# Block 1's output product cut into pieces of one contraction tile between the mLSTM heads, with the gate sums and first scores moved into the last attention unit

## The chip, the cores and the metric

The kernel runs on one NeuronCore of one Trainium2 chip. The metric is the device time of one execution in microseconds, the median of several runs. The engines are TensorE (matmuls, PE in the profile), VectorE (DVE), ScalarE (ACT), GpSimd (POOL) and SyncE (SP), which issues the DMAs of the weights. Each engine executes its own instructions in the order in which they are written; between engines there are only counting semaphores.

## The reference: two blocks, of which the first matters here

The input is one sequence of 256 tokens of width 1024. Block 1 is a hybrid layer, cut here to its core:

```
proj = rms_norm(x, g_mix_pre) @ w_in      # q,k,v of 8 attention heads; q,k,v,o and two gates of 4 mLSTM heads
att  = moba_attention(rope(aq), rope(ak), av)                  # causal softmax, 256 tokens
hm   = mlstm_chunkwise(q_m, k_m, v_m, ig, lf)                  # 4 heads of value width 128
hm   = rms_norm_per_head(hm) * g_mlstm_out * sigmoid(mo)
mixed = concat([att, hm])                                      # 512 + 512 columns
x = x + rms_norm(mixed @ w_out, g_mix_post)
u = square(relu(rms_norm(x, g_mlp_pre) @ w_up)); x = x + rms_norm(u @ w_down, g_mlp_post)
```

Block 2 (two layers with modulation by `ada_w`, differential attention, a convolution and a gated MLP) follows. The change leaves it as it is.

## The kernel before: how the work is laid out

**Weights.** All big products are float32 in three passes: a weight chunk of up to four contraction tiles (128 x 4 x 512, 1 MB) is loaded into `raw`, ScalarE writes its rounded high part `hi` (function `split` of ScalarE, line 797), VectorE writes the rest `lo` (`split` of VectorE, line 1115), and TensorE multiplies hi*hi, lo*hi and hi*lo (line 422). The three buffers form a ring of three slots, so `split` of chunk c waits until the product of chunk c-3 is finished (semaphore `mm_done`), and is called two chunks ahead of use (`LEAD = 2`). A chunk is 4 contraction tiles x 4 output tiles x 3 passes = 48 matmuls. The output product `mixed @ w_out` is chunks 12 to 15: 12 and 13 hold the contraction tiles of the attention half for output columns 0 to 511 and 512 to 1023 (the "halves" of the output), 14 and 15 those of the mLSTM half. Chunks 16 and later belong to `w_up`.

**Attention units.** Eight heads ("units", the loop `for i in range(UNITS + 1)`) go through a pipeline: `scores` (PE into bank 0), `softmax_max` (DVE), `exps` (ACT), `probs` (DVE), `turn` (PE transposes into bank 1), `take_turned` (ACT copies bank 1), `apply_v` (PE into bank 2), a copy (DVE, line 1335), `high` (ACT, `att_hi`) and `low_of_heads` (DVE, `att_lo`). The chunks of the input projection fill the units 0 to 6; units 7 and 8 have none.

**mLSTM heads.** For each of four heads h:

- `m_scores(h)`, PE: one matmul broadcasts the gate rows into bank 1 (line 624), two form the scores in bank 0 (lines 628 and 629).
- `m_exps(h)`, ACT: copy of bank 1 (`bcA`), then, after DVE's `m_args(h)`, the exponentials `sA` and `emA`.
- `m_weights(h)`, DVE: mask and product with the scores, lines 1351 and 1352.
- `m_sums(h)`, PE: four matmuls into bank 2, lines 637 to 640.
- `m_out(h)`, DVE: lines 1361 to 1364, ending in `hmA`. It frees bank 2.
- `m_norm(h)`, ACT, and `head_squares()`, PE (line 553): the square, its sum over the head, then Ln and Exp (`rstd`), later `act_hi` (line 863).
- `m_final(h)`, DVE: lines 1370 and 1374, then `act_lo` (line 1163).

On DVE the loop runs `m_args(h+1)`, `m_weights(h+1)`, `m_out(h)`, `m_final(h-1)`. On ACT it runs `m_exps(h+1)`, `m_norm(h-1)`. Before the change, TensorE does the whole chunk 12 after the sums of head 0, and chunk 13 after those of head 3; ScalarE and VectorE `split` chunks 14 and 15 at the same two places (`fill_at = {0: 0, MH: 1}`). Then come the chunks 14 and 15.

**What follows the product.** On ACT: `split(16)`, `split(17)`, then the squares of the output product (`post_norm`). On DVE: `split(16)`, one piece of the modulation product (`ada_piece`, lines 1134 and 1136), `split(17)`, another such piece, then `add_squares` (line 1394). On PE: `sum_squares_late` (lines 501 and 506) waits for `add_squares`; then four warm-up matmuls, the norm of `x`, and the product with `w_up`.

```
            for c in groups[("out", 0)][1][1:] + groups[("out", 1)][1][1:]:
                advance(c)
            post_norm("out", pcols("g_mix_post"))
```

Of the kernel before, what the change touches and what calls it, by code (L numbers as in the profile page):

```python
# [25 lines left out]
P = 128  # L26
S = 256
TT = S // P
# [4 lines left out]
CK = 4  # L33
RING = 3
LEAD = 2
EPS = 1e-6
EPS_SUB = 1e-5
QK = 64
# [132 lines left out]
def two_blocks(nc, t, consts, out):  # L171
# [48 lines left out]
    with ExitStack() as ctx:  # L220
# [8 lines left out]
        def sem(name):  # L229
            if name not in sems:  # L230
                sems[name] = nc.alloc_semaphore(name)
            return sems[name]
# [106 lines left out]
        fill_at = {0: 0, MH: 1}  # L339
# [49 lines left out]
        def _(pe):  # L389
# [209 lines left out]
            for i in range(UNITS + 1):  # L599
                if i < len(todoA):  # L600
                    name, j = todoA[i]
                    chunk(name, j, act_hi, act_lo, token_major=name in (("in", 2), ("in", 4)))
                if i + 1 < UNITS:
                    scores(qk1, i + 1)
                if i < UNITS:
                    turn(pA[:, i % 2, :])
                u = i - 1
                if u == 0:
                    pe.wait_ge(sem(freed(("in", 2))[0]), freed(("in", 2))[1])
                if u >= 0:  # L610
                    apply_v(ptA[:, u % 2, :], v1, u * QK, QK, QK * (u % 2), u % 2 == 1)


            wait("gate_rows_ready")
            b = bank(0)
            for tt in range(TT):
                ins = pe.transpose(b[:, 4 * tt:4 * tt + 4], gate[:, 5, tt * P:tt * P + P], ident[0:4, 0:4])
            full(ins, 0)
            for g in (3, 4):
                pe.wait_ge(sem(freed(("in", g))[0]), freed(("in", g))[1])  # L620

# [20 lines left out]
            m_scores(0)  # L642
            for h in range(MH + 1):
                if h + 1 < MH:
                    m_scores(h + 1)
                if h < MH:
                    m_sums(h)
                if h in fill_at:
                    chunk(("out", fill_at[h]), 0, att_hi, att_lo, ready=None if fill_at[h] else "act_ready")
                if h:  # L650
                    head_squares()

            for half in range(2):
                chunk(("out", half), 1, act_hi, act_lo, ready=None if half else "act_ready")
# [123 lines left out]
        def _(act):  # L778
# [132 lines left out]
            for i in range(UNITS + 1):  # L911
                if i < len(todoA):
                    name, j = todoA[i]
                    split(groups[name][1][j] + LEAD)
                if i + 1 < UNITS:
                    exps(i + 1, sA, pA)
                if i < UNITS:
                    take_turned(ptA[:, i % 2, :])
                if i < len(todoA) and j == 1:
                    if name[1] == 2:  # L920
                        evacuate(name, v1[:, :, :])
                    elif name[1] == 3:
                        evacuate(name, mqk[:, :, :])
                    elif name[1] == 4:
                        evacuate(name, mv[:, :, :])
                if i >= 2 and i % 2 == 0:
                    h = i // 2 - 1
                    high(hf[:, h % 2, :], att_hi[:, h, :], "of_ready", "act_hi_ready")

# [15 lines left out]
            m_exps(0)  # L945
            evacuate(("in", 5), mo[:, :, :], other(ACT.Tanh), 0.5)
            for h in range(MH + 1):
                if h in fill_at:
                    split(groups[("out", fill_at[h])][1][0] + LEAD)
                if h + 1 < MH:  # L950
                    m_exps(h + 1)
                if h:
                    m_norm(h - 1)
# [139 lines left out]
        def _(dve):  # L1093
# [227 lines left out]
            for i in range(UNITS + 1):  # L1321
                if i < UNITS:
                    probs(i, pA)
                if i == 0:
                    gate_rows()
                if i < len(todoA):
                    name, j = todoA[i]
                    advance(groups[name][1][j])
                if i + 1 < UNITS:
                    softmax_max(i + 1, sA)  # L1330
                if i % 2 == 1 and i >= 3:
                    low_of_heads(i // 2 - 1)
                if i >= 2 and i % 2 == 0:
                    h = i // 2 - 1
                    v(dve.tensor_copy(hf[:, h % 2, :], full(2)[:, 0:S]), "bank2_free")
                    v.settle()
                    dve.sem_inc(sem("of_ready"), 1)
            low_of_heads(UNITS // 2 - 1)
            link(dve.tensor_copy(acol[:].rearrange("p t h -> p (t h)"), full(0)[:, 0:8]), "bank0_free")

# [37 lines left out]
            m_args(0)  # L1378
            m_weights(0)
            for h in range(MH + 1):  # L1380
                if h in fill_at:
                    split(groups[("out", fill_at[h])][1][0] + LEAD)
                if h + 1 < MH:
                    m_args(h + 1)
                    m_weights(h + 1)
                if h < MH:
                    m_out(h)
                if h:
                    m_final(h - 1)
# [211 lines left out]
```

## Time and profile before

| | us |
|---|---|
| median of 3 runs | 1171.54 |
| lowest, highest | 1170.97, 1173.06 |
| the profiled execution, its time | 1168.2 |
| the profiled execution, its span | 1166.4 |
| PE busy / DVE busy / ACT busy in the span | 1113.2 / 815.4 / 525.8 |
| mean granted clock of TensorE | 0.981 of full speed |

The span runs from the first to the last instruction; the rest of the execution's time (1.8 us) lies around it. TensorE is busy nearly all the time, so what a change is worth is read where TensorE waits or runs at a lower granted clock. The part that the change touches lies between 115 and 190 us.

### The profile page before, as it was taken

The page shows a single profiled execution, that of the slowest core. Times are in us where ns is not written, and L with a number is a line of the kernel's source. Part 1 is how long each engine was busy: PE and PEld are TensorE (multiplying, and loading weights), DVE is VectorE, ACT ScalarE, POOL GpSimd, SP SyncE. Part 2 cuts the span into 40 slices and gives each one's busy share as a digit, 9 for nine tenths or more (in the row PEclk, how much of TensorE's full clock was granted, in tenths as well). Part 3 has the DMA queues.
Part 4 walks back from the last instruction along what each step waited for, and adds up shares of the span by engine and source line. Part 5 has one row for each costly group of instructions (what it writes and reads, how often), then busy time and mean ns, then how long its engine had stood idle before and what let it go on. Part 6 is the DMA issues. An engine that isn't in the chain of part 4 may idle for free.

```text
span 1166.4 us, 19617 instructions
## 1 busy us (share of the span) xinstructions
PE 1113.2 (95%) x8436; PEld 1049.9 (90%) x8436; DVE 815.4 (70%) x1089; ACT 525.8 (45%) x605; POOL 12.1 (1%) x26
## 2 busy tenths in 40 slices
PE   5999888999999899989999999999998999999998
PEld 5878677999999798978999999999897899999998
DVE  5965677777665799864788787768989277566452
ACT  4544445565333534544553434345346255444432
POOL 4000000000000000000000000000000000000000
PEclk8999889999999999989999999999999999999998
DMA  6543233887987154413879998955442275676550
GB/s 209 181 130 129 103 111 105 297 304 267 329 296 242 62 191 146 145 37 129 287 247 308 325 295 317 333 179 182 159 157 82 72 235 192 223 231 204 184 177 37
DMA packets 131494, 228.61 MB, mean 196 GB/s; under 512 B 5925, under 2 KB 59539, under 8 KB 131409
## 3 DMA queue, kind: packets, MB, share of 16 engines
q1 hardware_dynamic: 130404, 227.11, 57.8%
q8 instruction: 66, 1.08, 0.4%
q0 software_dynamic: 672, 0.06, 0.1%
q10 hardware_dynamic: 333, 0.21, 0.1%
q14 instruction: 19, 0.16, 0.0%
HBM read 226.30 MB, written 1.05 MB: 195 GB/s over the span
## 4 chain that ended last, share of the span: by engine, by line
PE 72%; DVE 19%; ACT 5%; issue 3%; DMA 1%; DVEq 0%; SPq 0%; ACTq 0%
PE mm L422 63%; DVE cacc L1195 5%; DVE lo L1115 5%; ACT hi L797 3%; PE pv L479 2%; PE mm L461 1%; DVE ada_acc L1136 1%; PE pa L506 1%; DVE sB L1203 1%; DMA raw<-in_w_out_dram 1%; DVE hf L1409 1%; DVE pB L1492 1%; PE pa L493 1%; DVE qk L1219 0%; DVE x L1414 0%
## 5 line engine op out<-in xcount | busy, mean ns | idle before, releaser
L422 PE MATMUL mm<-act_hi,hi 128*128 128x256 f32 x1760 | 491.6, 283 | 9.4 <-ACT act_hi L859 6.7
L422 PE MATMUL mm<-act_hi,lo 128*128 128x256 f32 x1760 | 486.0, 280 | 0.0
L1115 DVE TENSOR_TENSOR lo<-raw,hi 128x2048 fp32r<-128x2048 f32 (+1 forms) x160 | 361.8, 2265 | 172.1 <-ACT hi L797 170.8
L422 PE MATMUL mm<-act_lo,hi 128*128 128x256 f32 x1760 | 468.4, 279 | 0.0
L797 ACT ACTIVATE hi<-raw 128x2048 fp32r<-128x2048 f32 (+1 forms) x160 | 301.4, 1889 | 217.8 <-PE mm L422 167.4
L422 PEld LDWEIGHTS mm<-act_hi,hi 128*128 128x128 f32 x1760 | 332.0, 189 | 15.7 <-issue 8.9
L422 PEld LDWEIGHTS mm<-act_hi,lo 128*128 128x128 f32 x1760 | 332.0, 189 | 0.8 <-issue 0.7
L422 PEld LDWEIGHTS mm<-act_lo,hi 128*128 128x128 f32 x1760 | 321.0, 188 | 0.0
L422 PE MATMUL mm<-u_hi,hi 128*128 128x256 f32 x608 | 170.3, 280 | 0.0
L422 PE MATMUL mm<-u_hi,lo 128*128 128x256 f32 x608 | 169.7, 279 | 0.0
L422 PE MATMUL mm<-u_lo,hi 128*128 128x256 f32 x608 | 169.6, 279 | 0.0
L422 PEld LDWEIGHTS mm<-u_hi,lo 128*128 128x128 f32 x608 | 114.3, 188 | 0.0
L422 PEld LDWEIGHTS mm<-u_hi,hi 128*128 128x128 f32 x608 | 114.3, 188 | 0.0
L422 PEld LDWEIGHTS mm<-u_lo,hi 128*128 128x128 f32 x608 | 114.3, 188 | 0.0
L1136 DVE SCALAR_TENSOR_TENSOR ada_acc<-ada_raw,ca,ada_acc 128x1024 f32<-128x1024 f32 x84 | 107.6, 1280 | 1.3 <-DVE ada_acc L1136 0.3
L1195 DVE SCALAR_TENSOR_TENSOR cacc<-cu,convw,cacc 128x256 f32<-128x256 f32 x240 | 98.9, 477 | 2.4
L1163 DVE TENSOR_TENSOR u_lo<-sq,u_hi 128x512 fp32r<-128x512 f32 (+1 forms) x30 | 25.0, 834 | 35.2 <-ACT u_hi L983 18.6
L1066 ACT ACTIVATE sq<-mm 128x512 f32<-128x512 f32 x22 | 13.1, 597 | 61.0 <-PE mm L422 61.0
L422 PE MATMUL mm<-on,raw 128*128 128x256 f32 x128 | 33.5, 421 | 7.5 <-DVE on L1498 7.5
L422 PEld LDWEIGHTS mm<-on,raw 128*128 128x128 f32 x128 | 27.2, 215 | 12.7 <-issue 8.2
L870 ACT ACTIVATE pB<-sB,small 128x128 f32<-128x128 f32 (+1 forms) x32 | 14.3, 449 | 50.4 <-DVEq L1207 50.4
L863 ACT ACTIVATE u_hi<-sq 128x512 fp32r<-128x512 f32 x22 | 13.9, 632 | 44.5 <-DVEq L1552 44.5
(245 smaller groups left out, 976.5 us busy)
## 6 DMA issues: line engine op xcount, KB each, us to landing
ada_raw<-in_ada_w_dram SPq DMA_DIRECT2D x96, 512.0 KB, 5.9
raw<-in_w_ffn_in_dram SPq DMA_DIRECT2D x88, 512.0 KB, 5.8
raw<-in_w_in_dram SPq DMA_DIRECT2D x40, 1024.0 KB, 5.1
raw<-in_w_ffn_out_dram SPq DMA_DIRECT2D x20, 1024.0 KB, 6.3
raw<-in_w_up_dram SPq DMA_DIRECT2D x16, 1024.0 KB, 6.3
raw<-in_w_down_dram SPq DMA_DIRECT2D x16, 1024.0 KB, 7.3
raw<-in_w_out_dram SPq DMA_DIRECT2D x12, 1024.0 KB, 5.1
raw<-in_w_in_dram SPq DMA_DIRECT2D x16, 512.0 KB, 5.2
```

The lines of the kernel that those rows point to most:

```text
L422: ins = pe.matmul(o, w[:, kk, fs], a[:, k, :], start=(k == 0 and i == 0 and f % 2 == 0), stop=(ends and i == len(pairs) - 1), skip_group_c ...
L461: ins = pe.matmul(mm[:, b0 + tt, :], a[:, k, tok], w[:, kk, :], start=(k == 0 and i == 0), stop=(ends and i == 2), skip_group_check=True)
L479: ins = pe.matmul(b[:, f:f + 1], ada_acc[:, i % 2, f * P:(f + 1) * P], ones[:, 0:1], start=(f == 0), stop=True, skip_group_check=True)
L493: ins = pe.matmul(pa[:, 0:S], ones, sq[:, k, :], start=(k == 0), stop=(k == KD - 1))
L797: a(act.activation(hi[:, c % RING, 0:nk, :], raw[:, c % RING, 0:nk, :], ACT.Copy), "hi_done")
L863: a(act.activation(dst, src, ACT.Copy, scale=scale), done)
L870: a(act.activation(p[:, i, lo_:hi_], s[:, i, lo_:hi_], ACT.Exp, scale=-1.0, bias=small[:, 2 + 2 * i + q:3 + 2 * i + q], accum_out=small[:, ...
L1066: a(act.activation(sq[:, 0:2, :], complete((l, "ffn", g))[:, 0, :], other(ACT.Silu)), "silu_gate_ready")
L1115: v(dve.tensor_tensor(lo[:, c % RING, 0:nk, :], raw[:, c % RING, 0:nk, :], hi[:, c % RING, 0:nk, :].bitcast(F32), ALU.subtract), "lo_done")
L1136: link(dve.scalar_tensor_tensor(out=acc, in0=w, scalar=ca[:, 1, k:k + 1], in1=acc, op0=ALU.mult, op1=ALU.add), "ada_used")
L1163: ins = dve.tensor_tensor(d_lo, src, h, ALU.subtract)
L1195: v(dve.scalar_tensor_tensor(out=cacc[:, k, :], in0=src, scalar=w, in1=cacc[:, k, :], op0=ALU.mult, op1=ALU.add), name)
```

## The change

TensorE: in the last attention unit, after `turn(7)`, it now does the gate transposes, and `m_scores(0)`, ahead of both `apply_v` calls; between these stands the first piece of the output product. `out_piece(half, j, ks)` does contraction tiles `ks` of chunk 12 + half + 2j, 12 matmuls each. The remaining pieces stand between the heads, and the two mLSTM chunks alternate tile by tile. ScalarE and VectorE split chunk 14 in the last attention unit and chunk 15 after `m_exps(3)` and `m_weights(3)`. ScalarE does `m_exps(0)` ahead of `high` of the last attention pair; VectorE does the copies of the gate sums (`acol`) and `m_args(0)` ahead of the copy of that pair, and `m_weights(0)` behind it. What comes behind the product is unchanged.

```diff
-        fill_at = {0: 0, MH: 1}
...
+            def out_piece(half, j, ks):
+
+                name = ("out", half)
+                g, ids = groups[name]
+                slot, acts = ids[j] % RING, ((att_hi, att_lo), (act_hi, act_lo))[j]
+                if 0 in ks:
+                    begin(name, j)
+                for kk in ks:
+                    if half == 0:
+                        wait("act_ready")
+                    ends = j == 1 and kk == CK - 1
+                    for tiles in ((0, 1), (2, 3)):
+                        ins = tile_products(2 * (g % 2), slot, kk, CK * j + kk, tiles, acts, ends)
+                        if ends and half and tiles[0] == 0:
+                            ins.then_inc(sem("half_done"), 1)
+                if CK - 1 in ks:
+                    ins.then_inc(sem("mm_done"), 1)
+
             for i in range(UNITS + 1):
...
                 if i < UNITS:
                     turn(pA[:, i % 2, :])
+                if i == UNITS - 1:
+                    wait("gate_rows_ready")
+                    b = bank(0)
+                    for tt in range(TT):
+                        ins = pe.transpose(b[:, 4 * tt:4 * tt + 4], gate[:, 5, tt * P:tt * P + P], ident[0:4, 0:4])
+                    full(ins, 0)
+                    for g in (3, 4):
+                        pe.wait_ge(sem(freed(("in", g))[0]), freed(("in", g))[1])
+                    m_scores(0)
...
                     apply_v(ptA[:, u % 2, :], v1, u * QK, QK, QK * (u % 2), u % 2 == 1)
...
-            m_scores(0)
-            for h in range(MH + 1):
+                if i == UNITS - 1:
+                    out_piece(0, 0, (0,))
+
+            fill = [((0, 0, (1, 2)),), ((0, 0, (3,)), (1, 0, (0,))), ((1, 0, (1, 2)),), ((1, 0, (3,)), (0, 1, (0,)))]
+            for h in range(MH):
                 if h + 1 < MH:
                     m_scores(h + 1)
-                if h < MH:
-                    m_sums(h)
-                if h in fill_at:
-                    chunk(("out", fill_at[h]), 0, att_hi, att_lo, ready=None if fill_at[h] else "act_ready")
+                m_sums(h)
+                for piece in fill[h]:
+                    out_piece(*piece)
                 if h:
                     head_squares()
-
+            out_piece(1, 1, (0,))
             for half in range(2):
-                chunk(("out", half), 1, act_hi, act_lo, ready=None if half else "act_ready")
+                out_piece(half, 1, (1,))
+            head_squares()
+            for kk in (2, 3):
+                for half in range(2):
+                    out_piece(half, 1, (kk,))
...
                 if i + 1 < UNITS:
                     exps(i + 1, sA, pA)
+                if i == UNITS - 1:
+                    split(groups[("out", 0)][1][0] + LEAD)
                 if i < UNITS:
                     take_turned(ptA[:, i % 2, :])
+                if i == UNITS:
+                    m_exps(0)
...
             for h in range(MH + 1):
-                if h in fill_at:
-                    split(groups[("out", fill_at[h])][1][0] + LEAD)
                 if h + 1 < MH:
                     m_exps(h + 1)
+                if h == 2:
+                    split(groups[("out", 1)][1][0] + LEAD)
                 if h:
                     m_norm(h - 1)
...
                     low_of_heads(i // 2 - 1)
+                if i == UNITS:
+                    split(groups[("out", 0)][1][0] + LEAD)
+                    link(dve.tensor_copy(acol[:].rearrange("p t h -> p (t h)"), full(0)[:, 0:8]), "bank0_free")
+                    m_args(0)
                 if i >= 2 and i % 2 == 0:
                     h = i // 2 - 1
                     v(dve.tensor_copy(hf[:, h % 2, :], full(2)[:, 0:S]), "bank2_free")
                     v.settle()
                     dve.sem_inc(sem("of_ready"), 1)
+
+            m_weights(0)
             low_of_heads(UNITS // 2 - 1)
...
             for h in range(MH + 1):
-                if h in fill_at:
-                    split(groups[("out", fill_at[h])][1][0] + LEAD)
                 if h + 1 < MH:
                     m_args(h + 1)
                     m_weights(h + 1)
+                if h == 2:
+                    split(groups[("out", 1)][1][0] + LEAD)
                 if h < MH:
                     m_out(h)
```

Where two places of the program stand, in the order of instructions on an engine (line numbers differ between the two versions). First TensorE in the last attention unit, before; `cst,pA` is `turn(7)`, `ptA,v` are `apply_v(6)` and `apply_v(7)`, `cst,gate` the gate transposes, `gate,cst` and `mqk` are `m_scores`:

```order
L538 MATMUL pv<-cst,pA 128x128 [waits bank1_free,probs_ready]
L538 MATMUL pv<-cst,pA 128x128 x2
L545 MATMUL pv<-ptA,v 64x256 [waits bank2_free,bank1_free]
L546 MATMUL pv<-ptA,v 64x128
L545 MATMUL pv<-ptA,v 64x256 [waits bank1_free]
L546 MATMUL pv<-ptA,v 64x128
L617 MATMUL pv<-cst,gate 128x4 [waits bank0_free,gate_rows_ready]
L617 MATMUL pv<-cst,gate 128x4
L624 MATMUL pv<-gate,cst 128x512 [waits bank1_free,group_free0,group_free1]
L628 MATMUL pv<-mqk 128x256 [waits bank0_free]
L629 MATMUL pv<-mqk 128x128
```

The same place in the change:

```order
L537 MATMUL pv<-cst,pA 128x128 [waits bank1_free,probs_ready]
L537 MATMUL pv<-cst,pA 128x128 x2
L648 MATMUL pv<-cst,gate 128x4 [waits bank0_free,gate_rows_ready]
L648 MATMUL pv<-cst,gate 128x4
L600 MATMUL pv<-gate,cst 128x512 [waits bank1_free,group_free0,group_free1]
L604 MATMUL pv<-mqk 128x256 [waits bank0_free]
L605 MATMUL pv<-mqk 128x128
L544 MATMUL pv<-ptA,v 64x256 [waits bank2_free,bank1_free]
L545 MATMUL pv<-ptA,v 64x128
L421 MATMUL mm<-att_hi,hi 128x256 [waits act_ready,lo_done,group_free0]
```

The gate transposes and the scores of head 0 have moved ahead of both `apply_v`, and the first piece of the output product (its first row is the last one shown) stands between these.

VectorE around the outputs of heads 2 and 3, before; `lo<-raw,hi` is `split`, `hmA` ends `m_out`, `cols,rstd` begins `m_final`:

```order
L1352 SCALAR_TENSOR_TENSOR pA<-pv,sA 128x384 [waits bank0_full,dve_step]
L1361 TENSOR_TENSOR hf<-pv,emA 128x256 [waits bank0_free,bank2_full]
L1362 SCALAR_TENSOR_TENSOR hf<-pv,hf 128x256 [waits dve_step]
L1363 RECIPROCAL hf<-hf 128x256 [waits dve_step]
...
L1163 TENSOR_TENSOR act_lo<-hf,act_hi 128x256 [waits act_hi_ready]
L1115 TENSOR_TENSOR lo<-raw,hi 128x2048 [waits hi_done,act_ready]
L1370 SCALAR_TENSOR_TENSOR hf<-hmA,cols,rstd 128x256 [waits rstd_ready]
L1374 SCALAR_TENSOR_TENSOR hf<-mo,hf 128x256 [waits group_free1,dve_step]
```

The same engine and place in the change:

```order
L1357 SCALAR_TENSOR_TENSOR pA<-pv,sA 128x384 [waits bank0_full,dve_step]
L1140 TENSOR_TENSOR lo<-raw,hi 128x2048 [waits bank0_free,hi_done]
L1366 TENSOR_TENSOR hf<-pv,emA 128x256 [waits bank2_full]
L1367 SCALAR_TENSOR_TENSOR hf<-pv,hf 128x256 [waits dve_step]
L1368 RECIPROCAL hf<-hf 128x256 [waits dve_step]
...
L1188 TENSOR_TENSOR act_lo<-hf,act_hi 128x256 [waits act_hi_ready]
L1375 SCALAR_TENSOR_TENSOR hf<-hmA,cols,rstd 128x256 [waits rstd_ready,act_ready]
L1379 SCALAR_TENSOR_TENSOR hf<-mo,hf 128x256 [waits group_free1,dve_step]
```

The split of chunk 15 has moved from ahead of the last `m_final` to between the weights of head 3 and `m_out(2)`.

## Rows read from the trace of the kernel before

**Rows 1.** The page's first line: the span.

```profile
span 1166.4 us, 19617 instructions
```

**Rows 2.** Windows: busy us (instructions) by engine, then granted clock, DMA share, GB/s.

```profile
119.50:122.50 3.00, 2.58 (x12) 1.24 (x12) 0.91 (x3) 1.28 (x3) 0.00 (x0) 1.00 0.30 122
126.50:129.00 2.50, 2.50 (x8) 2.12 (x8) 0.60 (x1) 2.35 (x3) 0.00 (x0) 0.50 0.00 0
143.50:156.00 12.50, 8.45 (x28) 6.65 (x27) 8.80 (x16) 4.54 (x11) 0.00 (x0) 0.50 0.00 1
174.00:188.00 14.00, 10.66 (x44) 7.80 (x44) 7.14 (x15) 4.65 (x9) 0.00 (x0) 1.00 0.37 134
...
899.50:903.40 3.90, 0.49 (x3) 0.09 (x1) 3.90 (x10) 3.66 (x5) 0.00 (x0) 0.68 0.00 0
903.40:906.00 2.60, 2.28 (x6) 1.86 (x7) 0.57 (x2) 0.03 (x1) 0.00 (x0) 0.50 0.00 0
```

**Rows 3.** Timeline of PE: start, us, line, tiles, [idle before, releaser].

```profile
122.66 0.70 PE L628 MATMUL pv<-mqk 64*128 64x256 f32 x2 [0.58 <-DVE acol L1339]
137.03 0.70 PE L637 MATMUL pv<-pA,mv 128*128 128x256 f32 x2
138.69 0.70 PE L553 MATMUL pa<-sq,cst 128*128 128x256 f32 x2
150.95 1.19 PE L637 MATMUL pv<-pA,mv 128*128 128x256 f32 x2 [3.02 <-DVE hmA L1364]
153.64 1.06 PE L553 MATMUL pa<-sq,cst 128*128 128x256 f32 x2
```

**Rows 4.** The chain that ended last, pieces in order of time: start, us, what.

```profile
154.70 6.68 PE mm L422 x48
161.81 5.62 PE mm L422 x48
173.88 1.10 PE pa L501 x4
174.99 1.74 PE pa L506 x8
```

**Rows 5.** Timeline of ACT.

```profile
119.50 0.49 ACT L874 ACTIVATE ptA<-pv 128x384 f32<-128x384 f32 x1 [0.83 <-PE pv L538]
161.84 0.48 ACT L833 ACTIVATE rstd<-pa,small 128x256 f32<-128x256 f32 x1 [1.09 <-PE pa L553]
163.78 0.42 ACT L863 ACTIVATE act_hi<-hf 128x256 fp32r<-128x256 f32 x1 [1.01 <-DVE hf L1374]
164.11 1.90 ACT L797 ACTIVATE hi<-raw 128x2048 fp32r<-128x2048 f32 x1
167.50 1.92 ACT L797 ACTIVATE hi<-raw 128x2048 fp32r<-128x2048 f32 x1 [1.49 <-PE mm L422]
```

**Rows 6.** Timeline of DVE.

```profile
147.67 0.42 DVE L1361 TENSOR_TENSOR hf<-pv,emA 128x256 f32<-128x256 f32 x1
150.38 0.42 DVE L1364 TENSOR_TENSOR hmA<-pv,hf 128x256 f32<-128x256 f32 x1
160.55 2.29 DVE L1115 TENSOR_TENSOR lo<-raw,hi 128x2048 fp32r<-128x2048 f32 x1 [1.45 <-ACT hi L797]
162.81 0.48 DVE L1370 SCALAR_TENSOR_TENSOR hf<-hmA,cols,rstd 128x256 f32<-128x256 f32 x1
166.11 2.29 DVE L1115 TENSOR_TENSOR lo<-raw,hi 128x2048 fp32r<-128x2048 f32 x1 [1.45 <-ACT hi L797]
168.32 0.75 DVE L1134 TENSOR_SCALAR ada_acc<-ada_raw,ca 128x1024 f32<-128x1024 f32 x1
169.53 2.29 DVE L1115 TENSOR_TENSOR lo<-raw,hi 128x2048 fp32r<-128x2048 f32 x1 [0.46 <-ACT hi L797]
171.74 1.28 DVE L1136 SCALAR_TENSOR_TENSOR ada_acc<-ada_raw,ca,ada_acc 128x1024 f32<-128x1024 f32 x1
173.05 0.69 DVE L1394 TENSOR_TENSOR sq<-sq 128x512 f32<-128x512 f32 x1
```

More of the change, by code:

```diff
@@ L598, in _ @@
             full(ins, 2)
[L599 to L620, printed above, removed]
             def m_scores(h):
@@ new lines, in _ @@
+            for i in range(UNITS + 1):
+                if i < len(todoA):
+                    name, j = todoA[i]
+                    chunk(name, j, act_hi, act_lo, token_major=name in (("in", 2), ("in", 4)))
+                if i + 1 < UNITS:
+                    scores(qk1, i + 1)
+                if i < UNITS:
+                    turn(pA[:, i % 2, :])
+                if i == UNITS - 1:
[7 more added lines that the diff above has]
+                    m_scores(0)
+                u = i - 1
+                if u == 0:
+                    pe.wait_ge(sem(freed(("in", 2))[0]), freed(("in", 2))[1])
+                if u >= 0:
+                    apply_v(ptA[:, u % 2, :], v1, u * QK, QK, QK * (u % 2), u % 2 == 1)
+                if i == UNITS - 1:
+                    out_piece(0, 0, (0,))
@@ L910, in _ @@
             a(act.activation(gate[:, 2, :], gate[:, 2, :], ACT.Ln, bias=1.0), "softplus_ready")
[L911 to L928, printed above, removed]
             def m_exps(h):
@@ L943, in m_norm @@
                 high(hf[:, h % 2, :], act_hi[:, 4 + h, :], "of_ready", "act_hi_ready")
-            m_exps(0)
+            for i in range(UNITS + 1):
+                if i < len(todoA):
+                    name, j = todoA[i]
+                    split(groups[name][1][j] + LEAD)
+                if i + 1 < UNITS:
+                    exps(i + 1, sA, pA)
+                if i == UNITS - 1:
+                    split(groups[("out", 0)][1][0] + LEAD)
+                if i < UNITS:
+                    take_turned(ptA[:, i % 2, :])
+                if i == UNITS:
+                    m_exps(0)
+                if i < len(todoA) and j == 1:
+                    if name[1] == 2:
+                        evacuate(name, v1[:, :, :])
+                    elif name[1] == 3:
+                        evacuate(name, mqk[:, :, :])
+                    elif name[1] == 4:
+                        evacuate(name, mv[:, :, :])
+                if i >= 2 and i % 2 == 0:
+                    h = i // 2 - 1
+                    high(hf[:, h % 2, :], att_hi[:, h, :], "of_ready", "act_hi_ready")
             evacuate(("in", 5), mo[:, :, :], other(ACT.Tanh), 0.5)
             for h in range(MH + 1):
-                if h in fill_at:
-                    split(groups[("out", fill_at[h])][1][0] + LEAD)
                 if h + 1 < MH:
                     m_exps(h + 1)
+                if h == 2:
+                    split(groups[("out", 1)][1][0] + LEAD)
                 if h:
@@ L1320, in _ @@
             link(dve.memset(gate[:, 7, :], 0.0))
[L1321 to L1339, printed above, removed]
             def m_args(h):
@@ L1376, in m_final @@
                 v.settle()
-            m_args(0)
+            for i in range(UNITS + 1):
+                if i < UNITS:
+                    probs(i, pA)
+                if i == 0:
+                    gate_rows()
+                if i < len(todoA):
+                    name, j = todoA[i]
+                    advance(groups[name][1][j])
+                if i + 1 < UNITS:
+                    softmax_max(i + 1, sA)
+                if i % 2 == 1 and i >= 3:
+                    low_of_heads(i // 2 - 1)
+                if i == UNITS:
+                    split(groups[("out", 0)][1][0] + LEAD)
+                    link(dve.tensor_copy(acol[:].rearrange("p t h -> p (t h)"), full(0)[:, 0:8]), "bank0_free")
+                    m_args(0)
+                if i >= 2 and i % 2 == 0:
+                    h = i // 2 - 1
+                    v(dve.tensor_copy(hf[:, h % 2, :], full(2)[:, 0:S]), "bank2_free")
+                    v.settle()
+                    dve.sem_inc(sem("of_ready"), 1)
             m_weights(0)
+            low_of_heads(UNITS // 2 - 1)
             for h in range(MH + 1):
-                if h in fill_at:
-                    split(groups[("out", fill_at[h])][1][0] + LEAD)
                 if h + 1 < MH:
```

## The prediction

> **What bounds the kernel now.** I read the page first, then the chain that ended last, then the timelines of the three engines around the change, then windows for the granted clock. The span is 1166.4 us [rows 1]. The chain is TensorE for most of its length, so outside the changed stretch every microsecond by which the product with `w_up` starts later should stay to the end.
>
> In the changed stretch TensorE doesn't bound. Between the heads it waits for VectorE: 3.02 us before the sums of head 3, until `hmA` of head 2 is written [rows 3]. And it runs at half clock: 0.50 from 126.5 to 129.0 and again from 143.5 to 156.0 [rows 2]. What half clock costs is read from pairs of equal work: the sums of a head take 1.66 us at full clock (137.03 to 138.69) and 2.69 us at half (150.95 to 153.64) [rows 3]; a chunk that begins at half clock takes 6.68 us, one at full clock 5.62 us [rows 4]. One piece of the change is a quarter of a chunk, 1.405 us at full clock.
>
> The place that decides is the end. The product ends at about 173.0 us, but the sum of squares starts at 173.88 [rows 4], and it is VectorE that it waits for. Followed back on VectorE without a hole above 0.5 us: `add_squares` at 173.05, modulation piece from 171.74, split of chunk 17 from 169.53, modulation piece from 168.32, split of chunk 16 from 166.11 [rows 6]; that split waits for ScalarE's half of it at 164.11, which runs behind `act_hi` of head 3 at 163.78 [rows 5], and this behind `m_final(3)` at 162.81 [rows 6]. So the sum of squares starts 173.88 - 162.81 = 11.07 us after `m_final(3)` starts, however early the product itself ends, as long as it ends in that time. The only slack in it is the 0.46 us that VectorE waits for the split of chunk 17 [rows 6], since ScalarE can begin that only when chunk 14's product is done (167.50 [rows 5]).
>
> **Step 1, the last attention unit.** ScalarE is free 0.83 us before its copy of bank 1 at 119.50 [rows 5], so at 118.67. Now the split of chunk 14 (1.90) is ahead of this copy (0.49): it ends at about 121.0. The gate broadcast on TensorE uses bank 1 and waits for it; TensorE is done with the transposes and gate transposes at 119.7 and idles 1.3 us. It then broadcasts (1.05). On VectorE the split of chunk 14 (2.2) stands ahead of the `acol` copy, so the scores of head 0 start at 123.0 where they started at 122.66 [rows 3]. What is queued behind them: both `apply_v` (0.8 each) and the first piece (1.4), and VectorE's copy of bank 2 waits for the second `apply_v`, with `m_weights(0)` behind that copy. Worked out: 123.0 + 0.86 + 0.8 + 1.4 + 0.8 = 126.9; copy 0.42 and weights 1.16: 128.6. The sums of head 0 begin about 3 us later than before. Most of it is given back, since the split of chunk 14 no longer stands between heads 0 and 1 on either engine: I find `m_out(0)` about 0.5 us late.
>
> **Step 2, the heads.** They stay a serial loop of VectorE and ScalarE, and pieces on TensorE don't shorten it. The split of chunk 15 now stands between `m_weights(3)` and `m_out(2)`. `m_out(2)` ran from 147.67 to 150.80; with the split's 2.2 us and some 0.7 us of waiting for ScalarE's half of it ahead, it ends at about 153.8. TensorE waits for it with the sums of head 3: start 153.9 instead of 150.95. What TensorE has ahead of that ends sooner: sums of head 2 from about 144.0 (1.66), two pieces (2.81), a short wait and the head sum of head 1 (0.63), to about 149.5. So it idles about 4.4 us.
>
> **Step 3, the last head's norm.** Before, the split of chunk 15 (160.55 plus 2.2) stood right ahead of `m_final(3)` [rows 6], and `rstd`, begun at 161.84 [rows 5], was ready at the same time. The split is gone from there, but the last head sum now comes late on TensorE: behind the sums of head 3 (1.66) stand two pieces (2.81), a head sum (0.63), three pieces (4.22) and the head sum itself (0.63): 153.9 + 9.95 = 163.85. From the start of Ln to `m_final(3)` it was 162.81 - 161.84 = 0.97 [rows 5, 6]: `m_final(3)` starts at 164.9 instead of 162.81, 2.1 us later.
>
> **Step 4, the end.** The product ends at about 163.85 + 4 x 1.405 = 169.5, some 3.5 us earlier than before. But the sum of squares starts at 164.9 + 11.07 - 0.46 = 175.5, which is 1.6 us **later**. (The 0.46 goes, since ScalarE's split of chunk 17 is finished at about 170.2, before VectorE asks for it.) TensorE idles about 6 us there, where it idled 0.9.
>
> **Step 5, the clock.** After the 3.7 us for which TensorE waits near 900 us the clock is 0.50 for the next 2.6 us and the stretch with the gap itself has a mean of 0.68 [rows 2]. Both new gaps (4.4 and 6 us) are longer. After the first, the sums of head 3 cost 2.69 - 1.66 = 1.03 more, and the following pieces 6.68 - 5.62 = 1.06 more; all of this is ahead of the last head sum: +2.1. After the second, the sum of squares, 2.84 us at full clock [rows 4], costs at the ratio 2.69 / 1.66 another 1.8, and a little of the warm-up matmuls behind it: +2.0. Bounds of this term: nothing, if the clock holds, and about +5 if half clock lasts into the first matmuls of `w_up`; I take 2.0, because before the clock was 1.00 from 174 to 188 with gaps of up to 1.7 us [rows 2], so it comes back there. In step 1 the half-clock stretch of before (126.5 to 129.0) delayed nothing, since VectorE's split came last; now one between 122 and 127 would delay `m_weights(0)` by 1.0. Bounds 0 and 1.0; I take 0.5.
>
> Part 4 of the Trainium skill's page TensorE: Matmul & The Clock Gate says that transposes don't count as activity for the clock in the way matmuls do. The stretch 119.5 to 122.5 of before kept 1.00 with `apply_v` and the broadcast in it [rows 2]; in the change transposes and the broadcast alone stand there, which no row of before shows. By that rule the last term would be 1.0 instead of 0.5, and the sum 6.7.
>
> **Sum:** 1.6 + 2.1 + 2.0 + 0.5 = +6.2 us on the profiled execution's 1168.2 (span 1166.4 plus 1.8 around it), so 1174.4. The median of the runs is 3.3 us above that execution; against it I forecast 1171.54 + 6.2 = **1177.7 us**. The DMAs give nothing: chunks 17 and 18 load earlier, behind splits that come earlier, but no wait for them lies on this chain. Work on TensorE is the same, matmul for matmul.
>
> **Rivals.** A measurement tells about 0.2% (2.3 us) from no change.
>
> - *The clock holds* (the pieces between heads keep TensorE busy enough, and the gaps are not long enough). Then only 1.6 us remain: 1173.1, within 0.2%. For it: pieces now stand in the stretch from 143.5 to 156. Against it: the gaps themselves grow. Chance 0.14.
> - *The early split of chunk 15 is hidden*, because ScalarE has done its half in time and the sums of head 3 start at 151: then `m_final(3)` starts about 161.9, the end is 1.4 us earlier, 1170.1 at full clock, still within 0.2%. The row of `m_out(2)` shows VectorE at work without a hole on both sides, so I give it 0.03.
> - *Faster: the sum of squares follows the product.* If VectorE's chain of two splits and two modulation pieces were not what the sum of squares waits for, the product's earlier end would count: -3.5 us, 1168.0. It decides from the point at which `m_final(3)` starts before 160.5. Against it: VectorE's chain was the later one already. Chance 0.05.
> - *Half clock lasts longer*, through the norm into the first chunks of `w_up`, or in two stretches among the heads: +9.5 us, 1181. The gaps of the norm (up to 1.7 us) come right behind the long one. Chance 0.18.
>
> My forecast has 0.60. The likeliest case alone: 1175 to 1180. The range takes in the held clock and most of the longest: 1173.0 to 1181.0. Faster 0.05; within 0.2% 0.17; slower 0.78.
>
> **What the profile of the change would show.** Right, if: PE idles over 5 us before the sum of squares (line of `sum_squares_late`), released by DVE's `sq` add; PE idles about 4 us before the sums of head 3, released by `hmA`; the last `m_final` starts near 165 to 168; the clock shows 0.50 after both gaps; and the product ends before the 173.0 of before, or about there where half clock hits it. Wrong, if ScalarE's split of chunk 14 doesn't hold up the broadcast, if the last head sum is done by 161, or if the clock stays 1.00 behind the gap at the end.

## The result, and the profile after

| | before | after |
|---|---|---|
| median | 1171.54 us (7 runs, 1170.97 to 1173.06) | 1179.77 us (7 runs, 1176.44 to 1182.02) |
| profiled execution, time and span | 1168.2, 1166.4 us | 1180.19, 1178.3 us |
| mean granted clock | 0.981 | 0.975 |

The ratio is 1.0067 with a 95% interval of 1.0051 to 1.0082: slower by 7.9 us. I had forecast 1177.7 us, range 1173.0 to 1181.0.

The page of the change; the instructions are as many as before, and PE is busy 7 us longer (1120.3 against 1113.2) with the same matmuls, which is the clock:

```profile
span 1178.3 us, 19617 instructions
PE 1120.3 (95%) x8436; PEld 1055.7 (90%) x8436; DVE 815.8 (69%) x1089; ACT 525.8 (45%) x605; POOL 12.0 (1%) x26
```

The five longest waits of PE from 118 to 181 us (total us, times, longest); before, over the same stretch of the program, the first was 0.9 us and the second 4.7 us in two times:

```profile
PE pa L500 <- DVE sq L1421: 5.7, 1, 5.7
PE pv L613 <- DVE hmA L1369: 4.5, 1, 4.5
PE pv L537 <- DVE pA L1330: 1.4, 1, 1.4
PE pv L600 <- ACT ptA L896: 0.9, 1, 0.9
PE pv L604 <- DVE pA L1357: 0.8, 1, 0.8
```

VectorE in the change, the rows that answer to [rows 6]:

```profile
156.94 0.42 DVE L1369 TENSOR_TENSOR hmA<-pv,hf 128x256 f32<-128x256 f32 x1
...
169.46 0.48 DVE L1375 SCALAR_TENSOR_TENSOR hf<-hmA,cols,rstd 128x256 f32<-128x256 f32 x1 [2.90 <-ACT rstd L857]
...
172.77 2.29 DVE L1140 TENSOR_TENSOR lo<-raw,hi 128x2048 fp32r<-128x2048 f32 x1 [1.45 <-ACT hi L819]
174.97 0.75 DVE L1159 TENSOR_SCALAR ada_acc<-ada_raw,ca 128x1024 f32<-128x1024 f32 x1
175.76 2.29 DVE L1140 TENSOR_TENSOR lo<-raw,hi 128x2048 fp32r<-128x2048 f32 x1
177.97 1.28 DVE L1161 SCALAR_TENSOR_TENSOR ada_acc<-ada_raw,ca,ada_acc 128x1024 f32<-128x1024 f32 x1
179.28 0.69 DVE L1421 TENSOR_TENSOR sq<-sq 128x512 f32<-128x512 f32 x1
```

The reader is to see two things. Behind the last `m_final` (169.46) VectorE works without a hole to the add of squares, except for the wait for ScalarE's half of chunk 16 that it had before; and the second split no longer waits. TensorE had ended the product at 174.4 and starts the sum of squares at 180.12:

```profile
157.51 1.19 PE L613 MATMUL pv<-pA,mv 128*128 128x256 f32 x2 [4.46 <-DVE hmA L1369]
...
180.12 2.04 PE L500 MATMUL pa<-sq,cst 128*128 128x256 f32 x4 [5.68 <-DVE sq L1421]
181.96 3.02 PE L505 MATMUL pa<-sq,cst 128*128 128x256 f32 x8
```

Windows of the change: the last unit, the sums of head 3, the gap at the end with the sum of squares behind it (the last figures are granted clock, DMA share, GB/s):

```profile
120.50:129.40 8.90, 8.03 (x24) 5.12 (x24) 3.01 (x4) 2.19 (x5) 0.00 (x0) 0.50 0.55 190
157.50:160.20 2.70, 2.69 (x9) 2.34 (x9) 1.33 (x3) 0.72 (x2) 0.00 (x0) 0.50 0.97 380
175.00:180.00 5.00, 0.00 (x0) 0.00 (x0) 4.90 (x5) 1.99 (x5) 0.00 (x0) 0.74 0.60 185
180.00:184.60 4.60, 4.48 (x12) 3.62 (x13) 0.00 (x0) 0.00 (x0) 0.00 (x0) 0.54 1.05 405
```

The product with `w_up` starts at 196.47 instead of 188.21: +8.26, of which 0.42 was there before the changed instructions. So the changed stretch accounts for 7.8 us, about what the medians show (7.9). The two profiled executions differ by 11.9 us: 8.3 up to the start of that product, and 3.6 behind it, in code that the change leaves alone. Half clock at differing places in that code was part of it (last section).

### The profile page after: what moved, and what is told of

It is laid out like the page before. It is cut to its first block, busy times and chain, and to the rows that moved or that the text cites. A ratio compares the mean times of both kernels' runs of the same rounds, so it can differ in the third digit from the quotient of the medians.

```text
span 1178.3 us, 19617 instructions
## 1 busy us (share of the span) xinstructions
PE 1120.3 (95%) x8436; PEld 1055.7 (90%) x8436; DVE 815.8 (69%) x1089; ACT 525.8 (45%) x605; POOL 12.0 (1%) x26
## 4 chain that ended last, share of the span: by engine, by line
PE 70%; DVE 19%; ACT 6%; issue 3%; DMA 2%; DVEq 0%; SPq 0%; ACTq 0%
PE mm L421 60%; DVE lo L1140 5%; DVE cacc L1220 5%; ACT hi L819 3%; PE pv L478 2%; PE mm L460 1%; DMA raw<-in_w_out_dram 1%; DVE ada_acc L1161 1%; PE pa L505 1%; PE pa L492 1%; DVE sB L1228 1%; DVE pB L1519 1%; PE pa L500 1%; DVE qk L1244 0%; DVE hf L1202 0%
## 5 line engine op out<-in xcount | busy, mean ns | idle before, releaser
L1091 ACT ACTIVATE sq<-mm 128x512 f32<-128x512 f32 x22 | 13.2, 599 | 65.7 <-PE mm L421 65.7
```

What stands on the lines that cost most here:

```text
L1091: a(act.activation(sq[:, 0:2, :], complete((l, "ffn", g))[:, 0, :], other(ACT.Silu)), "silu_gate_ready")
```

## The experiments

All were timed in turns with the kernel before; each ratio is to that kernel's runs of the same job, whose medians were 1171.79, 1172.25 and 1172.03 us. Where two versions ran in different jobs, their difference is taken from the ratios, and it is uncertain by 2 to 3 us, since each ratio has an interval of 1.3 to 2.3 us to either side. So the profiles are compared too: in each I count from the same VectorE instruction ahead of all that was moved (the first of `softmax_max` in the last unit, at 116.27 us before and 116.69 in the change) to the first matmul of `w_up`. So counted, the change takes 7.8 us more than before. The expectations speak of four theories. A: the loss comes from the pieces and splits between the heads, through VectorE's chain behind the product, the late sums and half clock behind the gaps. B: it comes from the last attention unit. C: it comes from the alternation of the two chunks of the second half, by which chunk 14 is done later. D concerns the late head sum and the split of chunk 15: whether one of them is the link that binds, or they only change places with another wait.

**1. The last attention unit alone**, on the kernel before: the edits of the diff in `for i in range(UNITS + 1)`, without the piece and without the split of chunk 14.

```diff
+                if i == UNITS - 1:
+                    wait("gate_rows_ready")
+                    b = bank(0)
...
+                    m_scores(0)
...
+                if i == UNITS:
+                    m_exps(0)
```

> The kernel before with only the last attention unit changed: gate transposes and the scores of head 0 ahead of both value products on TensorE, the first exponentials ahead on ScalarE, the gate sums' copy and first arguments ahead on VectorE; no piece of the output product is moved and the splits of chunks 14 and 15 stay. Theory A (the loss is made by the pieces and splits between the heads and by VectorE's chain behind the product): within 1 us of before, 1170.5 to 1172.5. Theory B (the reordered unit makes the loss, through waits for bank 1 and for the gate sums): 1176 to 1180, about what the whole change cost.

Measured: 1172.50 us, ratio 1.0007 (0.9991 to 1.0023). By itself the reordered unit makes no difference that the timings could tell; a loss of up to 2.7 us stays possible. Its profile has one: counted as above, `hmA` of head 0 comes 2.1 us later than before and `w_up` 2.9 us later. Theory B can't hold the 7.9 us, but the unit isn't free.

**2. The pieces and splits between the heads alone**: the change, with the unit put back.

```diff
-                if i == UNITS - 1:
-                    out_piece(0, 0, (0,))
-            fill = [((0, 0, (1, 2)),), ((0, 0, (3,)), (1, 0, (0,))), ((1, 0, (1, 2)),), ((1, 0, (3,)), (0, 1, (0,)))]
+            m_scores(0)
+            fill = [((0, 0, (0, 1, 2)),), ((0, 0, (3,)), (1, 0, (0,))), ((1, 0, (1, 2)),), ((1, 0, (3,)), (0, 1, (0,)))]
```

> The change with the last attention unit put back as it was; pieces between the heads as in the change (three of them behind the sums of head 0), chunk 14 split with head 0 as before, chunk 15 split ahead of the output of head 2. Theory A: +5 us on before, about 1177 (the change less 1.5 to 3 us), TensorE idle over 5 us ahead of the sum of squares. Theory B: 1171 to 1173.

Measured: 1177.04 us, ratio 1.0046 (1.0029 to 1.0063), +5.4 us (+5.1 in the profile), and its profile has the same two gaps:

```profile
PE pa L500 <- DVE sq L1417: 5.7, 1, 5.7
PE pv L613 <- DVE hmA L1365: 4.7, 2, 4.5
```

Two thirds of the loss are here. The rest, about 2.5 us, goes with the unit (with its piece and the split of chunk 14, which were put back too). The intervals of the change and of this version overlap, so that this figure alone would not be safe; the profiles give 2.7 us, and experiments 9 and 10 again 2.5.

**3. The chain behind the product taken apart**, on the change.

```diff
-            for c in groups[("out", 0)][1][1:] + groups[("out", 1)][1][1:]:
-                advance(c)
+            split(groups[("out", 0)][1][1] + LEAD)
             post_norm("out", pcols("g_mix_post"))
+            split(groups[("out", 1)][1][1] + LEAD)
             normalise(pcols("g_mlp_pre"), 1, lambda k: hf[:, k % 4, :])
+            for c in groups[("out", 0)][1][1:] + groups[("out", 1)][1][1:]:
+                for j in range(pieces):
+                    if ada_pos[j] == c:
+                        ada_piece(j)
```

> The change, but the split of chunk 17 on ScalarE stands behind the squares of the output product, on VectorE behind the update of x, and both modulation pieces behind the norm. Theory A: the sum of squares starts within 2.5 us of the product's end, its stretch stays at full clock, and of the 8 us most come back: 1171.5 to 1173.5. Theory C (the product alternating between two chunks tile by tile is itself slower, or the late end of chunk 14 holds things up elsewhere): 1177 or more, since the product ends as late as in the change.

Measured: 1173.74 us, ratio 1.0011 (0.9999 to 1.0022). 6.6 us of 7.9 come back (by the ratios; 6.0 in the profiles). On each of the two engines one split, that of chunk 17, and on VectorE both modulation pieces, have left the chain; the split of chunk 16 stays ahead. The sum of squares follows the split of chunk 16 and the add, and at full clock it takes 2.8 us again. PE's rows:

```profile
177.37 1.10 PE L500 MATMUL pa<-sq,cst 128*128 128x256 f32 x4 [1.36 <-DVE sq L1422]
178.30 1.89 PE L505 MATMUL pa<-sq,cst 128*128 128x256 f32 x8
```

Theory C falls too as an explanation of the 7.9 us. That alternating between two chunks costs nothing by itself isn't shown: up to 2.6 us may be left.

**4. The same, on the kernel before**, where TensorE waits only 0.9 us at that place.

> The kernel before with the splits of chunk 17 and the modulation pieces moved behind the squares, the update and the norm, as in the version of the change that was run with this. In the kernel before, TensorE waits only 0.9 us ahead of the sum of squares, so at most that can be gained: 0 to 1 us faster than before, 1170.8 to 1172. If the moved modulation pieces hold up the loads of the first chunks of w_up or the product with them: 1173 or more.

Measured: 1171.86 us, ratio 1.0006 (0.9987 to 1.0025): no difference that could be told (0.8 us faster in the profile, up to `w_up`). So the chain is dear only when the product ends well ahead of it. The moved modulation pieces show no cost either, within the same interval.

**5. Warm-up matmuls in the gap at the end**, on the change: the clock's share there.

```diff
+            for _ in range(13):
+                pe.matmul(pv[1][:, 0:S], ident, cst[:, C_ID:C_ID + S], start=True, stop=True)
             for late in (True, False):
```

> The change with 13 further warm-up matmuls of 256 columns on TensorE between the end of the product and the sum of squares, about 5.6 us at full clock, in the gap where TensorE has nothing to do. Theory A with the clock's share as predicted (+2.0 us behind that gap): about 2 us faster than the change, 1177.5, with the sum of squares taking 2.8 us instead of 4.7. If the clock's share there is nothing: 1179.8. If the added matmuls outlast the gap: slower than that by what they outlast it.

Measured: 1179.19 us, ratio 1.0059 (1.0040 to 1.0078), which can't be told from the change. But the place itself shows the effect. The added matmuls (L679) fill the gap, and what follows runs at full clock:

```profile
174.12 5.78 PE L679 MATMUL pv<-cst 128*128 128x256 f32 x26
179.96 1.10 PE L500 MATMUL pa<-sq,cst 128*128 128x256 f32 x4
180.90 1.89 PE L505 MATMUL pa<-sq,cst 128*128 128x256 f32 x8
```

Where the change's sum of squares ran from 180.12 to 184.98, this one runs from 179.96 to 182.8, and the first matmul of `w_up` starts at 194.31 instead of 196.47. So half clock behind the gap costs 2.0 us in the trace (2.16 less the 0.16 by which this execution was ahead); the timing is too coarse to confirm it.

**6. Warm-up matmuls in the gap ahead of the sums of head 3**, on the change.

```diff
+                else:
+                    pe.wait_ge(sem("bank1_free"), n.seen("bank1"))
+                    for _ in range(10):
+                        pe.matmul(pv[1][:, 0:S], ident, cst[:, C_ID:C_ID + S], start=True, stop=True)
                 m_sums(h)
```

> The change with 10 further warm-up matmuls (4.3 us at full clock) on TensorE in the 4.5 us gap ahead of the sums of head 3. If half clock behind that gap costs what was predicted (2.1 us ahead of the last head sum, handed on to the end by the chain behind it): about 2 us faster than the change, 1177.7, with the sums of head 3 taking 1.66 us and the last normalisation starting 11.5 us after the output of head 2 instead of about 12. If the chain doesn't hand it on: 1179.8.

Measured: 1177.88 us, ratio 1.0042 (1.0025 to 1.0060), 1.9 us under the change by the medians, 2.9 by the ratios, with intervals that overlap. In the trace the sums of head 3 run at full clock (1.00 from 158.45 to 160.0), and the last `m_final` starts 10.7 us after the end of `hmA` of head 2, not 12.1: 1.4 us gained. Only 0.5 us of that is left at `w_up`, partly because the sum of squares took 5.5 us here, at half clock for longer than in the change (4.9). Two of its VectorE rows:

```profile
157.88 0.42 DVE L1373 TENSOR_TENSOR hmA<-pv,hf 128x256 f32<-128x256 f32 x1
...
169.02 0.48 DVE L1379 SCALAR_TENSOR_TENSOR hf<-hmA,cols,rstd 128x256 f32<-128x256 f32 x1 [2.90 <-ACT rstd L861]
```

**7. Chunk 15 split behind `m_out(2)`** on VectorE, on the change.

```diff
-                if h == 2:
-                    split(groups[("out", 1)][1][0] + LEAD)
                 if h < MH:
                     m_out(h)
+                if h == 2:
+                    split(groups[("out", 1)][1][0] + LEAD)
```

> The change, but VectorE splits chunk 15 behind the output of head 2 instead of ahead of it; ScalarE as in the change. Theory A: the output of head 2 ends about 3 us earlier, TensorE's gap ahead of the sums of head 3 shrinks from 4.5 to about 1.5 us, the last normalisation starts 3 us earlier, and half clock there mostly goes: 4 to 5.5 us faster than the change, 1174 to 1176. Theory D (the split only changes places with other waiting, since the last head sum is late behind the pieces anyway): within 1 us of the change, 1179 to 1181.

Measured: 1175.33 us, ratio 1.0039 (1.0023 to 1.0056). That is 3.3 us under the change by the ratios (4.4 by the medians of two different jobs, 3.6 in the profiles), a little less than expected. One pair of lines exchanged on one engine gives back some two fifths of the loss. Three of its waits:

```profile
PE pa L500 <- DVE sq L1421: 5.7, 1, 5.7
PE pa L492 <- ACT sq L864: 3.1, 4, 1.7
PE pv L613 <- DVE hmA L1369: 1.7, 1, 1.7
```

Ahead of the sums of head 3 the gap is 1.7 us. The one at the end stays, since all of it moves up together.

**8. Head sums earlier on TensorE**, on the change.

```diff
-                for piece in fill[h]:
-                    out_piece(*piece)
+                out_piece(*fill[h][0])
                 if h:
                     head_squares()
+                for piece in fill[h][1:]:
+                    out_piece(*piece)
...
             out_piece(1, 1, (0,))
-            for half in range(2):
-                out_piece(half, 1, (1,))
             head_squares()
-            for kk in (2, 3):
+            for kk in (1, 2, 3):
```

> The change, but on TensorE each head sum stands behind the first set of pieces after the head's sums instead of behind all, and the last one behind one piece of chunk 15 instead of three. Theory A: the last normalisation starts 1 to 1.5 us earlier (it then waits for the output of head 3, not for TensorE): 1 to 3 us faster than the change, 1177 to 1178.5. Theory D (the head sums are what is late): 4 us faster or more, 1176 or less.

Measured: 1180.06 us, ratio 1.0077 (1.0057 to 1.0097): **a miss of both theories**, no gain. The last `m_final` did come 2.3 us earlier as counted from `hmA` of head 2 (9.8 us instead of 12.1). But:

```profile
168.88 0.49 DVE L1374 SCALAR_TENSOR_TENSOR hf<-hmA,cols,rstd 128x256 f32<-128x256 f32 x1 [1.68 <-ACT rstd L856]
...
174.40 0.75 DVE L1158 TENSOR_SCALAR ada_acc<-ada_raw,ca 128x1024 f32<-128x1024 f32 x1
176.93 2.29 DVE L1139 TENSOR_TENSOR lo<-raw,hi 128x2048 fp32r<-128x2048 f32 x1 [1.78 <-ACT hi L818]
```

The split of chunk 17 waits 1.78 us. ScalarE can begin it only when chunk 14's product is done, and since the two chunks alternate, that is a piece before the end of all. The sum of squares starts 12.4 us after the last `m_final`, not 10.7, so most of what the head sum gained, the ring slot took back.

**9. All three corrections** (3, 7 and 8) on the change.

> The change with all three corrections: chunk 15 split behind the output of head 2, head sums ahead of the pieces, split of chunk 17 and modulation pieces out of the chain behind the product. Theory A: the product ends about 2.5 us earlier than in the kernel before and the sum of squares follows it within 1 us: 2 to 3.5 us faster than the kernel before, 1168.3 to 1169.8. If the pieces between the heads give nothing even when nothing holds up the end: 1171 to 1172.5, like before.

Measured: 1169.29 us, ratio 0.9984 (0.9971 to 0.9997): 1.9 us **faster than before** (0.6 in the profiles, up to `w_up`). Now the gaps of 4.5 and 5.7 us are gone, and PE waits 0.6 us ahead of the sum of squares.

**10. The same with the last attention unit put back.**

> The version with all three corrections, and the last attention unit put back as it was before the change. If the unit's reordering costs something of its own (its value products, first piece and scores ran at half clock for up to 9 us in the change's profile): 0.5 to 2 us faster than with all three corrections, 1167.3 to 1168.8. If the reordered unit helps: slower than 1169.3.

Measured: 1167.36 us, ratio 0.9963 (0.9948 to 0.9978): 4.3 us faster than before (4.1 in the profiles, up to `w_up`), and 2.5 us (by the ratios, whose intervals just touch) better than with the reordered unit. It is the fastest version measured. PE around the end of its product:

```profile
170.20 1.10 PE L500 MATMUL pa<-sq,cst 128*128 128x256 f32 x4 [0.60 <-DVE sq L1417]
171.14 1.89 PE L505 MATMUL pa<-sq,cst 128*128 128x256 f32 x8
```

The sum of squares starts at 170.20, where it started at 173.88 before [rows 4].

**Where the unit costs.** Versions 9 and 10 differ in the unit alone (with its piece and the split of chunk 14), ran in different jobs, and reach the same VectorE instruction ahead of it at 116.42 and 116.77. `hmA` of head 0 starts at 139.65 with the reordered unit and at 136.57 with the old one: 3.4 us more, counted from there. It isn't chance: in all seven profiles with the whole unit of the change, `hmA` of head 0 comes 3.2 to 3.7 us later than before, with the old unit 0.0 us in all three others. Windows of version 9, then of version 10, then of the unit alone (columns as above):

```profile
123.00:128.00 5.00, 4.85 (x16) 3.72 (x17) 0.64 (x4) 0.83 (x2) 0.00 (x0) 0.50 0.77 252
118.00:137.00 19.00, 14.94 (x54) 10.70 (x55) 7.76 (x18) 8.46 (x15) 0.00 (x0) 0.73 0.38 138
```

```profile
123.00:128.00 5.00, 3.99 (x13) 2.63 (x14) 1.78 (x5) 4.27 (x6) 0.00 (x0) 0.88 0.01 2
118.00:137.00 19.00, 15.29 (x76) 11.09 (x75) 11.05 (x21) 9.52 (x16) 0.00 (x0) 0.91 0.40 143
```

```profile
118.00:137.00 19.00, 17.12 (x64) 11.31 (x64) 8.44 (x21) 9.43 (x17) 0.00 (x0) 0.64 0.27 89
```

In all profiles the granted clock over 118 to 137 us orders by the unit (the same work lies up to 2.0 us later in some of them): with the old one 0.91 (before), 0.91 (experiment 4), 0.91 (version 10), 0.82 (experiment 2); with the reordered one 0.64 to 0.76 in eight kernels. PE's rows in the change:

```profile
121.41 2.04 PE L600 MATMUL pv<-gate,cst 4*128 4x512 f32 x2 [0.87 <-ACT ptA L896]
123.42 1.22 PE L604 MATMUL pv<-mqk 64*128 64x256 f32 x2
...
132.13 0.70 PE L604 MATMUL pv<-mqk 64*128 64x256 f32 x2 [0.77 <-DVE pA L1357]
...
132.98 1.20 PE L613 MATMUL pv<-pA,mv 128*128 128x256 f32 x2
```

The same place in version 9, then the scores of head 0 in version 10:

```profile
121.13 1.09 PE L600 MATMUL pv<-gate,cst 4*128 4x512 f32 x2 [1.31 <-ACT ptA L895]
123.15 1.22 PE L604 MATMUL pv<-mqk 64*128 64x256 f32 x2 [0.92 <-DVE acol L1397]
```

```profile
123.17 0.70 PE L604 MATMUL pv<-mqk 64*128 64x256 f32 x2 [0.59 <-DVE acol L1398]
```

The broadcast isn't what costs. It took 2.04 us in the change and 1.09 in version 9, yet the scores of head 0 start 6.73 us behind the same VectorE instruction in both: where the broadcast is short, they wait for `acol`, which stands behind VectorE's split of chunk 14. Half clock costs from the scores on. From 123.42 to 129.33 TensorE does the scores, an `apply_v` and the piece, 5.9 us where the prediction's figures at full clock give 3.1, and the second `apply_v`, `m_weights(0)` and the sums of head 0 hang behind it.

The lower clock there is shown: the first score matmul takes 1.22 us in all eight kernels with the reordered unit and 0.70 in the four with the old one. Why it is granted isn't: the order puts four gate transposes, a wait and the broadcast with 4 rows where `apply_v` stood, and no kernel separated these three. In three profiles half clock had begun still earlier, in the change's at 119.4, before TensorE's first moved instruction (120.16); by the figure of 6.73 us that early part cost nothing.

## Why the prediction was right, and where it was mis-sized

The forecast was +6.2 us and the medians give +8.2 on the 1171.54 (7.9 by the ratio). By place, from the profiles of before and after, with what had shifted by 0.42 us ahead of the change taken off:

| term | forecast | measured |
|---|---|---|
| `hmA` of head 0 (the unit) | +0.5 | +3.2 |
| from there to `hmA` of head 2 (the split of chunk 15) | +3.0 | +3.0 |
| from there to the last `m_final` (late head sum, clock) | +1.2 | +0.1 |
| from there to the sum of squares (the lost wait) | -0.46 | -0.4 |
| the sum of squares at half clock | +2.0 | +2.0 |
| sum | +6.2 | +7.8 |

The rows of before are [rows 3] for TensorE and [rows 6] for VectorE. Behind it nothing changes: from the end of the sum of squares to `w_up` it is 11.5 us in both profiles.

The sum came out closer than its terms. Two were off, in opposite directions: the unit by +2.7 us and the late head sum with its clock by -1.1. The path, the waits and the links of steps 2 to 5 are as forecast, but part of the nearness of the total is luck.

- **Step 1, the unit: the term that was mis-sized most.** I had taken 0.5 us within bounds of 0 to 1.0. Measured: +3.2 in the profiles, 2.5 by the timings of versions 9 and 10. The moves were read rightly (the scores start at 123.42, forecast 123.0 plus the 0.42 of earlier shift); what I took too short was half clock. I allowed it one stretch from 122 to 127, and in the change it lasts from 120.5 to 129.4. `m_weights(0)` ended at 132.1 where I had 128.6. Part 4 of the Trainium skill's page TensorE: Matmul & The Clock Gate, by which transposes don't count as activity for the clock in the way matmuls do, had spoken for the higher of two values (1.0 instead of 0.5). The direction agrees with the runs, the cause isn't shown by them, and both values were too small.
- **Step 2, the heads: right.** `m_out(2)` comes 3.0 us later against the unit's end, and TensorE waits 4.46 us (forecast 4.4). Experiment 7 shows the split as the cause: behind `m_out(2)` it leaves a wait of 1.7 us and gives back 3.3 us of 7.9.
- **Step 3, the last head's norm: right in kind, its clock term too large.** The last `m_final` waits 2.90 us for `rstd`. It starts at 169.46, later than the 165 to 168 that I had named, because of the unit. From `hmA` of head 2 it takes 12.1 us, not the 13.2 of my sum. Of my 2.1 us for half clock experiment 6 gives back 1.4: the sums of head 3 ran at 0.50, but from 160.1 to 165.0 the clock was 0.98, so that the pieces behind them paid next to nothing where I had put 1.06. The rest of that chain took 10.7 us (experiment 6), where I had 11.1.
- **Step 4, the end: right, and the main step.** The sum of squares starts 10.66 us after `m_final(3)` (forecast 10.61) and TensorE idles 5.68 (forecast about 6). Experiment 3 shows that the chain, not the product, sets it: -6.6 us with the split of chunk 17 and the two modulation pieces out of the way. The product itself ended at 174.4, where my figures gave 169.5, and 172.1 with the clock terms of step 5, and so not before the 173.0 that I had named as a sign; that cost nothing, since the chain ended later still.
- **Step 5, the clock: right behind the gap at the end.** 4.86 us instead of 2.85, and full clock with the gap filled (experiment 5).

The rivals. *The clock holds*: no, 0.50 behind both gaps. *The split is hidden*: no. *The sum of squares follows the product*: not in the change; its condition, a last `m_final` before 160.5 (my own figures give 159.8: 3.5 us off 173.88, less 10.61), was never near. But its reasoning was sound: with the chain shortened the product's end counts, and versions 9 and 10 are faster than before. *Half clock lasts longer*: not into `w_up`, as I had put it; but the same thing happened in the unit, and the result lies between this rival and my forecast.

What was missed lies in experiment 8: with the head sum early, the split of chunk 17 becomes the late link, for its ring slot. So what the early head sum is worth depends on whether that split is still in the chain. In the totals this can't be seen: alone the corrections 3, 7 and 8 give 6.6, 3.3 and -1.2 us by the ratios, together 9.7 (in the profiles 6.0, 3.6 and -0.5, together 8.4), and the uncertainty is larger than the difference. Whether version 9 needs the early head sum at all was not tried.

## What to carry to other kernels

Work put into the waits of an engine moves nothing if the stretch's end hangs on another engine's chain: follow that chain back from the instruction that the end waits for, and shorten it first. Here the pieces between the heads, with the old unit, lost 5.4 us while two splits and two modulation pieces stood between the last norm and the sum of squares, and won 4.3 us once one of the splits and both modulation pieces stood behind it and a split and a head sum had changed places. Where such pieces need something from the other engine, as the split of a chunk, its place in that engine's order can be worth as much as the pieces (3.3 us for two lines). And an order that ends in a long wait of TensorE pays beyond the wait, since what follows runs at half clock (2.0 us here behind 5.7).

## What the runs showed of the hardware

- Behind waits of TensorE of 4.5 and 5.7 us the next matmuls ran at a granted clock of 0.50 in every kernel that had them, and 5.8 us of small matmuls in place of the longer wait (experiment 5), or 4.5 us in place of the shorter (experiment 6), kept it at 1.00.
- Waits of 1.4 to 1.7 us didn't decide it by their length: before kept 1.00 from 118 to 123 us with 1.41 us of waiting in it, while the change ran from 119.4 at half clock behind a wait of 1.42 us. And behind 1.65 us the sums of head 2 ran at 0.53 before (142.93 to 145.5), behind 1.74 us those of head 3 at 1.00 in experiment 7 (154.07 to 155.6).
- Code that no kernel touched takes a different time in each execution: from the first matmul of `w_up` to the end it was 978.2 us before, 981.8 in the change, 984.1 in experiment 5 and 978.0 in experiment 2. The profile of before had granted clock 1.00 from 420 to 440 us after that matmul, the change 0.91. So two profiled executions may differ by 6 us for nothing that the edit did, and only stretches can be compared by trace.
